# 64 expert slots moved beside the last projection units of a one-core decoder step

## The reference, cut to what matters

```
xn   = rms_norm(x); proj = xn @ w_in                        # (tokens, 3328)
q, k = rope(proj[:, :512]), rope(proj[:, 512:1024]); v = proj[:, 1024:1536]; p_rw = proj[:, 1536:]
o_da = rms_norm(diff_attend(q, k, v))                       # 4 heads, two softmax maps
o_rw = rwkv_time_mix(p_rw, state)                           # 8 heads of 64, a recurrence
h    = x + concat(o_da, o_rw) @ w_out
hn   = rms_norm(h)
s    = (hn @ wq) . sub_keys                                 # 8 heads x 2 x 128 scores per token
pick 16 of 16x16 pairs per head -> 16 expert numbers, softmax gates
y    = h + sum_k gate_k * gelu(hn . u[e_k]) * v[e_k]        # 128 experts per token
out  = rms_norm(y)
```

## Time and profile before

| | |
|---|---|
| median of 3 runs | 3936.64 us (3932.21 to 3939.34) |
| the profiled execution | 3929.9 us, span 3928.1 us |
| granted TensorE clock, mean | 0.794 |
| PE / DVE / ACT / POOL busy | 2876.3 / 2599.3 / 1289.5 / 1367.6 us |
| DMA traffic | 1431.66 MB, mean 364 GB/s |
| first gather of a slot | 745.49 us after the span's start |

### The profile page before, as it was taken

One profiled execution on the slowest core, in us unless ns is written; L12 is line 12 of the kernel. 1 busy time (PEld: TensorE's weight loads), 2 busy tenths in 40 slices (PEclk: granted clock), 3 DMA queues, 4 the chain that ended last, 5 costly groups with the idle time before them and its releaser, 6 DMA issues.

```text
span 3928.1 us, 54696 instructions
## 1 busy us (share of the span) xinstructions
PE 2876.3 (73%) x20366; PEld 1348.2 (34%) x20366; DVE 2599.3 (66%) x5836; ACT 1289.5 (33%) x3597; POOL 1367.6 (35%) x1190
## 2 busy tenths in 40 slices
PE   6899999775678676766766776677576758866565
PEld 3654454342224232322332243224232315521111
DVE  2422456398568948884987598768866776446954
ACT  1311211334332524342434334433433224432232
POOL 1000000244334434443444343434343456533453
PEclk9999999887787787878777777878777667777565
DMA  8534524799999999999999999999999999999998
GB/s 312 196 142 172 194 73 166 307 420 420 422 419 402 420 422 410 419 409 420 413 418 402 419 412 411 385 419 412 393 410 393 375 343 414 405 408 422 416 408 355
DMA packets 254827, 1431.66 MB, mean 364 GB/s; under 512 B 27521, under 2 KB 45457, under 8 KB 110305
## 3 DMA queue, kind: packets, MB, share of 16 engines
q0 software_dynamic: 163232, 1162.26, 72.6%
q1 hardware_dynamic: 91328, 265.89, 17.9%
HBM read 1373.21 MB, written 54.85 MB: 364 GB/s over the span
## 4 chain that ended last, share of the span: by engine, by line
DMA 25%; DVE 17%; PE 16%; issue 5%; POOL 1%; ACT 1%; another core or an unknown queue 0%; SPq 0%; DVEq 0%; ACTq 0%; POOLq 0%
DMA pe_buf<-in_experts,pe_idx 24%; DVE pe_buf L2312 6%; PE pe_psO L1466 4%; PE pe_psH L1448 2%; PE pe_B L1412 2%; POOL pe_buf L1040 1%; PE pe_B L1365 1%; DVE pe_few L2082 1%; PE pe_B L1111 1%; PE pe_B L1304 1%; DMA op_w<-in_w_out 1%; PE pe_B L1395 1%; DVE pe_topi L2191 0%; PE pe_B L1118 0%; PE pe_psW L1436 0%
## 5 line engine op out<-in xcount | busy, mean ns | idle before, releaser
L1040 POOL DMA_INDIRECT pe_buf<-in_experts,pe_idx x1088 | 1281.2, 1178 | 2442.9 <-PE pe_psO L1466 1637.1
L2312 DVE CUSTOM_DVE_ANT_0 pe_buf<-pe_buf,pe_hnR 128x1024 f32<-128x1024 f32 x1088 | 1316.5, 1223 | 695.0 <-DMA pe_buf<-in_experts,pe_idx 647.4
L1466 PE MATMUL pe_psO<-pe_buf,pe_Z 128*32 128x256 f32 x8704 | 843.8, 485 | 631.6 <-ACT pe_Z L1744 599.4
L1738 ACT ACTIVATE pe_gelu<-pe_dot 128x1 f32<-128x1 f32 x1088 | 219.2, 201 | 1622.7 <-DVE pe_dot L2312 1570.2
L1466 PEld LDWEIGHTS pe_psO<-pe_buf,pe_Z 128*32 128x32 f32 x8704 | 215.2, 123 | 1299.0 <-ACT pe_Z L1744 993.5
L1448 PE MATMUL pe_psH<-pe_hn,pe_pick 128*128 128x512 f32 x544 | 415.8, 856 | 44.9 <-ACT pe_hnR L1720 41.3
L1077 PE MATMUL ip_B<-ip_w,ip_xT 128*128 128x512 f32 (+1 forms) x1008 | 430.4, 577 | 16.2 <-DMA ip_w<-in_w_in 16.2
L1744 ACT ACTIVATE pe_Z<-pe_gl,pe_gelu 128x8 f32<-128x8 f32 x1088 | 327.2, 301 | 43.3 <-PE pe_psO L1466 0.4
L1412 PE MATMUL pe_B<-op_wkr,pe_mix 128*128 128x512 f32 (+1 forms) x576 | 270.0, 613 | 9.5 <-DMA op_wkr<-scratch_wk_rows 9.4
L1077 PEld LDWEIGHTS ip_B<-ip_w,ip_xT 128*128 128x128 f32 x1008 | 190.0, 194 | 211.1 <-issue 205.6
L1448 PEld LDWEIGHTS pe_psH<-pe_hn,pe_pick 128*128 128x128 f32 x544 | 108.9, 247 | 175.6 <-issue 88.8
(11 more groups left out here) (344 smaller groups left out, 3600.6 us busy)
## 6 DMA issues: line engine op xcount, KB each, us to landing
op_wkr<-scratch_wk_rows SPq DMA_DIRECT2D x36, 2048.0 KB
ip_w<-in_w_in SPq DMA_DIRECT2D x18, 2048.0 KB, 9.0
op_w<-in_w_out SPq DMA_DIRECT2D x9, 2560.0 KB
pe_buf<-in_experts,pe_idx POOLq DMA_INDIRECT x1088
op_w<-in_w_out SPq DMA_DIRECT2D x9, 1024.0 KB
ip_w<-in_peer_wq SPq DMA_DIRECT2D x4, 2048.0 KB, 11.2
scratch_wk_rows<-wk_wkc SPq DMA_DIRECT2D x16, 512.0 KB, 6.0
tm_ps<-scratch_moved_rows SPq DMA_DIRECT2D x8, 896.0 KB
```

The source lines that it names most:

```text
L1040: pool.indirect_dma_start(buf[b][:], None, T["experts"], bass.IndirectOffsetOnAxis(ap=idx[:, t % 2, h * NJ + j:h * NJ + j + 1], axis=0)).t ...
L1466: last = nc.tensor.matmul(psO[32 * x:32 * x + 32, j // 4, :], Z[:, n % NZ, 24 - 8 * turn:56 - 8 * turn], buf[home[n]][:, D + x * QUART:D + ...
L1738: nc.scalar.activation(gelu[:, col:col + 1], dot[:, col:col + 1], ACT.Gelu_apprx_tanh).then_inc(f["gelu_done"], 1)
L2312: nc.vector.tensor_tensor_reduce(buf[b][:, 0:D], buf[b][:, 0:D], hnR[:, n // PH % 2, :], 1.0, 0.0, ALU.mult, ALU.add, dot[:, n % (NBUF + E ...
```

## The change

Four stages of fill now stand where three stood. Stage 2 holds only units 7 to 19 beside the front of tile 0; stage 3 has units 20 to 39 beside topk of tile 0 and the first 12 steps of the front of tile 1; stage 4 has units 40 to 62 beside the rest of that front and, new, the first 64 slots (`early`). These slots use three extra buffers in turn (numbers 9, 10, 11), since the nine ordinary ones are not free until slot 66 (`EARLY`). In this part the lags are gone: ScalarE gates a slot in the same slot's second step (`late`), and TensorE adds slot n-1 at slot n. Units from 40 on go to the single bank `psW`, and each waits until the unit before it has been taken out.

From slot 64 on, the fronts of tiles 2 to 5 are dealt over 112 slots each in place of 128 (`FRONT_BY`), and topk of tiles 1 to 4 over slots 66, 50, 34 and 18 to 120 in place of 2 to 120 (`TOPK_FROM`). The fronts of tiles 6 to 8 stand where they stood. The loads of tile 1's time mixing rows move from the front of tile 0 to the start of its own. With one more extra buffer there are still eleven in use from slot 66 to 240, ten to 496 and nine after.

```diff
-IP_HALF = IP.index(("unit", 5 * NG + 2, 0))
-ALONE = NU
-EXTRA = 2
-EXTRA_UNTIL = (2 * 128 - 16, 4 * 128 - 16)
+IP_A, IP_B = IP.index(("unit", 2 * NG + 6, 0)), IP.index(("unit", 5 * NG + 5, 0))
+ALONE = IP[IP_B][1]
+NEXT_A, GAP = 12, 18
+FILL_SLOTS = 64
+EARLY = FILL_SLOTS + 2
+EXTRA = 3
+EXTRA_UNTIL = (EARLY, 2 * 128 - 16, 4 * 128 - 16)
 
 FILL = (((("ip", (0, IP_FIRST)),),),
-        ((("ip", (IP_FIRST, IP_HALF)),), (("gap", 4), ("tm", 0), ("at", 0), ("op", 0))),
-        ((("ip", (IP_HALF, IP_STEPS)),), (("tm", 1), ("at", 1), ("op", 1)), (("topk", 0),)))
+        ((("ip", (IP_FIRST, IP_A)),), (("gap", 4), ("tm", 0), ("at", 0), ("op", 0))),
+        ((("ip", (IP_A, IP_B)),), (("gap", GAP), ("next", (0, NEXT_A))), (("topk", 0),)),
+        ((("ip", (IP_B, IP_STEPS)),), (("next", (NEXT_A, None)),), (("early", (0, FILL_SLOTS)),)))
+NEXT = (("tm", 1), ("at", 1), ("op", 1))
...
+FRONT_BY = (48, 32, 16, 0, 0, 0) + (LAST_OP_BY,)
+TOPK_FROM = (FILL_SLOTS + 2,) + tuple(by + 2 for by in FRONT_BY)
...
-    plan = []
+    plan = [0] * FILL_SLOTS
...
-        length = PER if t < len(DURING) - 1 else PER + LAST_OP_BY
+        length = (t + 1) * PER + FRONT_BY[t] - len(plan)
...
-        free = [NBUF + i for i in range(EXTRA) if n < EXTRA_UNTIL[i]] + list(range(NBUF))
+        free = [NBUF + i for i in range(EXTRA) if n < EXTRA_UNTIL[i]] + (list(range(NBUF)) if n >= EARLY else [])
...
+        def early(lo, hi):
+            for n in range(lo, hi):
+                slot(n)
+                yield
+                if late is not None:
+                    late(n)
+                yield
...
-        for n in range(TOTAL):
+        for n in range(FILL_SLOTS, TOTAL):
...
                     pool.wait_ge(ip["summed"], NT)
                     for i in range(2):
                         pool.wait_ge(wk_stored[i], 16 * PH)
+                if n == EARLY:
                     for i in range(2):
                         pool.wait_ge(ip_stored[i], stored_of(NU, i))
...
+                if 0 < n < FILL_SLOTS:
+                    v_sum(n - 1)
...
-                if n >= SUM_LAG:
+                if n - SUM_LAG >= max(FILL_SLOTS - 1, 0):
                     v_sum(n - SUM_LAG)
```

More of the change, by code:

```diff
@@ L12 @@
+import itertools
 from contextlib import ExitStack
@@ L219 @@
 TOPK_STEPS = 8 * PH // 2 + 6
-TOPK_FROM, TOPK_FROM_LAST, TOPK_TO = 2, 66, 120
+TOPK_TO = 120
 ACT_LAG, SUM_LAG = 1, 2
@@ L232, in steps_of @@
         return arg[1] - arg[0]
+    if stage == "next":
+        return sum(steps_of(i) for i in NEXT) - arg[0] if arg[1] is None else arg[1] - arg[0]
+    if stage == "early":
+        return 2 * (arg[1] - arg[0])
     if stage == "at":
@@ L244, in costs_of @@
             costs += [ip_cost(i) for i in range(*item[1])]
+        elif item[0] == "next":
+            costs += costs_of(NEXT)[item[1][0]:item[1][1]]
         else:
@@ L324, in topk_pulls, with run @@
     def topk_pulls(t, k):
-        first = TOPK_FROM if t < LAST - 1 else TOPK_FROM_LAST
+        first = TOPK_FROM[t]
         n = TOPK_TO - first
         return min(max(k + 1 - first, 0), n) * TOPK_STEPS // n - min(max(k - first, 0), n) * TOPK_STEPS // n
-    def run(slot, stage):
+    def run(slot, stage, late=None):
+        def early(lo, hi):
[5 more added lines that the diff above has]
+                yield
         def through(items):
             for kind, arg in items:
-                yield from range(arg) if kind == "gap" else stage[kind](arg)
+                if kind == "next":
+                    yield from itertools.islice(following, steps_of((kind, arg)))
+                elif kind == "early":
+                    yield from early(*arg)
+                else:
+                    yield from range(arg) if kind == "gap" else stage[kind](arg)
+        following = through(NEXT)
         for streams in FILL:
@@ L343, in run @@
                     raise ValueError("steps are left over")
+        if next(following, "end") != "end":
+            raise ValueError("steps are left over")
         front, choice = through([item for window in DURING for item in window]), None
-        for n in range(TOTAL):
+        for n in range(FILL_SLOTS, TOTAL):
             t, k = n // PER, n % PER
-            if k == 0 and t < LAST:
+            if (k == 0 or n == FILL_SLOTS) and t < LAST:
                 choice = stage["topk"](t + 1)
@@ L493, in peer @@
             e = Mem(nc, early, "pe")
-            e.sb("hold_kv", [P, 4 * D])
+            e.sb("hold_kv", [P, 2 * D])
             buf += [e.sb(f"buf{NBUF + i}", [P, 2 * D]) for i in range(EXTRA)]
@@ L786, in mix_in_time @@
                 for k in tm_labels(t):
+                    if k == 0 and t == 1:
+                        sp.wait_ge(op["scores_done"], NC)
+                        load_p(1)
                     if k == 2:
@@ L792, in mix_in_time @@
                             fold_stored()
-                        if t in (4, 6):
-                            sp.wait_ge(f["v_used"], 1 + max(n for n in range(TOTAL) if home[n] == NBUF + t // 2 - 2))
+                        if t in (2, 4, 6):
+                            sp.wait_ge(f["v_used"], 1 + max(n for n in range(TOTAL) if home[n] == NBUF + t // 2 - 1))
                         if t < LAST:
@@ L878, in project_out @@
                         sp.wait_ge(op["hn_stored"], 16 * (t + 1))
-                        if t + 1 < LAST:
+                        if 0 < t < LAST - 1:
                             load_moved(t + 1)
@@ L882, in project_out @@
                         sp.wait_ge(op["scores_done"], NC * t + NC - 1)
-                        if t + 1 < LAST:
+                        if 0 < t < LAST - 1:
                             load_kept(t + 1)
-                        else:
+                        elif t:
                             load_p(t + 1)
@@ L923, in slot @@
                 t, k = n // PER, n % PER
-                if n == 4:
+                if n == EARLY + 4:
                     project_stored(NU)
@@ L1758, in slot @@
                         repeat_hn(n // PH + 1, (h - 4) // 3)
-                if n >= ACT_LAG:
+                if n >= FILL_SLOTS + ACT_LAG:
                     gate(n - ACT_LAG)
@@ L1766, in _ @@
             junk = psW[:, 256:512]
-            run(slot, {"ip": project, "tm": mix_in_time, "at": attend, "op": project_out, "topk": topk})
+            run(slot, {"ip": project, "tm": mix_in_time, "at": attend, "op": project_out, "topk": topk}, gate)
             for n in range(TOTAL - ACT_LAG, TOTAL):
```

2 lines of the change are left out of this document (1 added, 1 removed).

## The result

The changed kernel takes 3973.85 us (median of 4 runs, 3961.79 to 3976.44), against 3934.43 us (4 runs, 3931.33 to 3939.34) for the kernel before on the same chip. The ratio is 1.0093, 95% interval 1.0069 to 1.0117: 39 us slower, where +15 was forecast. The profiled execution has a span of 3974.5 us, 46.4 us above the span before.

The account below looks back on a forecast made before the run. TensorE was taken to bound the fill and the DMA engines the slots. 3928.1 - 165 (gathers) + 130 (fill) + 50 (VectorE) = 3943 us of span; 3950 was said, between 3945 and 3952, the likeliest case ranging 3930 to 3995.

Parts of the forecast that it names:

- the case's own range: Whole kernel, likeliest case: slower by some, with waits 60 to 100 and loss 35 to 65; 3930 to 3995 us, chance 0.42.
- The gathers removed: Slots after the fill: 66 fewer gathers at 2.50 us each have to pass, 165 us less.
- The fill: Fill before the ordinary slots: 130 us longer from added TensorE work and waits, range 75 to 200, ending near 870 us.
- First, stage 2: Stage 2 of the fill: units leave, thinning the cover of tile 0's exchanges; TensorE waits 30 us, range 10 to 50.
- The single bank: Fill from unit 41 on: each unit waits until the one before is taken out; 22 waits, 15 us taken, at most 22.
- The slots without lags: Early slots in stage 4: about 18 uncovered slots wait 2.0 us each; 30 us taken, range 5 to 128.
- The ring: Three buffers for early slots: a 10.2 us round, 3.4 us a slot against 4.5 available, so on average not the limit.
- VectorE behind the fill: Slots from 64 on: squeezed choosing of experts puts VectorE behind the DMA pace; 50 us lost, range 20 to 90.
- A (cover holds): Fill and slots behind: engines run ahead and hide most waits, making the kernel faster; 3860 to 3885 us, chance 0.36.
- B (a chain, 4030): Stage 4: every early slot costs TensorE 2.0 us and the buffer round shows; 4030 us, chance 0.10 shared with D.
- C (the sums cancel): Whole kernel: fill and VectorE give back the 165 us within a few us; 3929 to 3944 us, chance 0.12.
- D: Stage 4: early gathers compete with the projection's weights for DMA; tens of us, chance 0.10 shared with B.

Follow-up runs that it names:

- e1: Changed kernel's new fill order and single bank without the 64 early slots, everything from slot 0 dealt as in the kernel before: 3967.37 us, ratio 1.0090.
- e2: As e1, but units 40 to 62 use the three rotating banks again: 3954.71 us, ratio 1.0055.
- e8: Changed kernel with two temporary buffers in place of three for the first 64 slots: 4054.07 us, ratio 1.0285.
- e3: Changed kernel with the products of slots 66 to 511 over half the columns, the rest left out: 3904.42 us, ratio 0.9929.
- e4: Kernel before the change with the products of slots 66 to 511 over half the columns, the rest left out: 3926.98 us, ratio 0.9992.
- e6: Changed kernel with the fronts of tiles 2 to 5 slowed while topk runs and catching up outside it: 3955.08 us, ratio 1.0055.
- e7: Changed kernel with 32 early slots in place of 64, fronts and topk dealt to match: 3935.24 us, ratio 1.0001.
- e5: Changed kernel with each single-bank unit taken out beside its own second half, one step earlier: 3966.88 us, ratio 1.0085.

## Why the prediction was right or wrong

**Direction and size.** Slower, 3950 forecast, 3974 measured, inside the case's own range. The change itself was forecast at +15 us and came at +39, so it was sized at less than half. The sum was 3943 us of span, 31.5 below the measured one. Step by step:

**The gathers removed: -165 us.** Right as an amount. When VectorE is relieved, the part behind gather 66 takes 3903.5 - 873.60 = 3029.9 us of span, 152.7 less than before.

**The fill: +130, measured +128.8.** Right in sum, in part by luck, and about right in its two halves: 45 of it was foreseen for the thinner cover and the bank, and e1 gives 37.4 for these; 85 for the slots, their work and their waits, and the rest, 128.8 - 37.4 = 91, is theirs. But one step inside it was wrong. "First, stage 2 ... I take 30 us" did not happen: TensorE's idle time from 95 us to the end of stage 2 is 21.8 us (252 - 230.18), with 20.5 us up to 446 us before, and the only large wait is the folds', as before. The loss was one stage later, in a place that I had not read: the turns of `x` of tiles 5 to 8 wait for VectorE, which now goes through topk of tile 0 beside them, 18.8 us in place of 4.2. I had counted the engines' cover for the work that was moved and not for what it was moved beside. Stage 4 was too short in the sum as well: 290 us of work and 45 of waits make 335, and it took 359, with 313 of them busy.

**The single bank: 15.** Measured 12.7 us of time and 19.9 us of fill (e2), 22.9 us of wait in the full version. The Trainium skill's rule ("Perfetto Trace Analysis", section "Optimizing Tensor Performance": independent groups should rotate through PSUM banks) agrees with the trace here: e1 on the single bank has 12.6 us of waits for it, e2 with the rotation none. With one wait for each of 22 units the prediction had 22 us by it; the full version's 22.9 us stand in 14 places, so the sum agrees and the count does not.

**The slots without lags.** The waits for `pe_Z` are 17.8 us in 7 places. The other part of the 91 us is work: TensorE's busy time in the fill grew by 79 us against the kernel before. The slots' sums and repeats are 61.2 us of it (40.1 and 21.1, 48 to 77 foreseen). The projection's 1008 instructions are another 15.8: 446.2 us busy (276.8 in three banks, 169.4 in the single one), where it was 430.4. The 368 on the single bank alone take 169.4 us with slots between them and 156.9 in e1 without, and the granted clock is 0.94 to 0.95 where it was 0.97 to 0.98. The sum had no term for a lower clock.

**The ring.** "On average the ring is not the limit" was right as an average and wrong as a reason to give it no price: e8 shows that one buffer fewer costs 80 us, and VectorE waited 133.4 us in 42 places for a gather in stage 4. That TensorE waited for gates at all, 17.8 us, may be a part of what three buffers cost. The round of 10.2 us was read where TensorE had nothing else to do. I did not test a fourth buffer, so what three buffers cost is open.

**VectorE behind the fill: +50, measured 82.6 lost, 66 to 70 of it by VectorE.** This is the term that was mis-sized, and it makes the whole difference between 3943 and 3974.5. The mechanism is shown: relief gives 69 us in one kernel and not over 4 in the other (e3, e4), shifting the load without changing it gives 15 to 19 (e6), and the loss grows with the squeeze, 3.5, 29 and 83 us with 0, 32 and 64 early slots (e1, e7). The sum per tile took means over each window and gave a credit of 8 slots run ahead. The load is not even: behind 100 us with VectorE full, TensorE was full for 20 at half clock, in time mixing (1010 to 1030 us). That the one brought about the other fits e3, where the part with a full TensorE falls with VectorE's relief, and the wait at 989 us shows one such step, but it was not tested by itself. Of the 71.4 us idle, 22.1 lie in windows with TensorE full. I had forecast the engine, not this second one. Nor does show what I took it for, DMA lost to VectorE at 88% busy, less than the 96% that cost nothing in the earlier trace rows: its share is lowest from 2455 to 2460 us (0.28), where TensorE is full at a clock of 0.50, right behind a wait of 8.57 us for `at_prob` from VectorE. Some 12 to 16 us of the 82.6 are left when VectorE is relieved; their cause stays open.

**Rivals.** A (cover holds) falls by the fill's end at 866 and by e1. B (a chain, 4030) falls: stage 4 waited 46 us in all, and the slots came at 5.6 us each. C (the sums cancel) is what happens with 32 slots, not with 64. D falls: the DMA share of stage 4 is 0.78, with room left.

**The signs named.** First gather 494 (near 510 said), last single-bank unit near 861 (850 to 890), DMA share in stage 4 0.78 (0.7 to 0.8), stage 4 idle 45.8 us (60 to 80 said: too much), VectorE above 95% with a DMA share near 0.85 for 180 us (0.90 over 900 to 1000, then broken by TensorE), and full DMA again only from the later tiles on.

## What to carry to other kernels

Work moved from a part bound by one engine into a slack part pays only while each piece costs less, in both parts, than it saves. Here 2.5 us are saved against 1.6 for each of the first 32 slots and 3.7 for each of the next 32, so the first half was worth it and the second was not; with the 37 us of the new order on top, the first half only breaks even (e7). Where an engine sits at 96% beside a full bottleneck there is no room for a squeeze of its other duties: here that cost 66 to 70 us. Spreading the load against the known peaks gave back 15 to 19 us (e6), and removing waits in the fill 7, not clear of noise (e5). For a ring of buffers, measure the round where the consumer is busy, not where it idles.
